# Branch B's head norms: the sum of squares by one product with a tile of ones, power and factor over 256 columns

## The reference, cut to what matters

```python
o_b = hgrn2_chunkwise(qb, 1.0 - f, vb, jnp.log(f)).astype(x.dtype)
o_b = rms_norm(o_b, hgrn_out_norm_g)          # over the 128 channels of each head
y_b = o_b.reshape(B, T, BRANCH_WIDTH) * jax.nn.silu(z_b)

def rms_norm(x, gain):
    xf = x.astype(jnp.float32)
    y = xf * lax.rsqrt(jnp.mean(xf * xf, axis=-1, keepdims=True) + EPS)
    return (y * gain.astype(jnp.float32)).astype(x.dtype)
```

## Time and profile before

| what | value |
|---|---|
| median of 3 runs | 1909.64 us (1907.76 to 1910.26) |
| profiled execution | 1908.92 us, span 1907.6 us |
| granted PE clock, mean | 0.998 of full |
| PE busy | 1890.0 us, 99% of the span |
| PE weight loads busy | 1857.5 us, 97% |
| DVE busy | 1174.7 us, 62% |
| ACT busy | 880.1 us, 46% |
| POOL busy | 323.6 us, 17% |
| PE on the chain that ended last | 92% |

### The profile page before, as it was taken

How to read it: one execution, slowest core, us unless ns; L and a number is a source line. 1 busy time by engine, 2 the same in 40 slices (tenths; PEclk the granted TensorE clock), 3 DMA queues, 4 the chain that set the end, 5 groups by cost and what they waited for, 6 DMA issues and landing times.

```text
span 1907.6 us, 37116 instructions
## 1 busy us (share of the span) xinstructions
PE 1890.0 (99%) x15758; PEld 1857.5 (97%) x15758; DVE 1174.7 (62%) x1709; ACT 880.1 (46%) x1265; POOL 323.6 (17%) x317
## 2 busy tenths in 40 slices
PE   9999999999999999999999999999999999999999
PEld 8999999999999999999999999999999999999987
DVE  7765665656554556755654766676467776655744
ACT  6544454544444444544454543446443333444543
POOL 3220110202110003400221243040011132110300
PEclk9999999999999999999999999999999999999999
DMA  7566555566666666666565565563564444666664
GB/s 262 165 211 182 158 154 165 167 188 191 197 191 195 198 190 188 194 204 193 196 232 195 177 217 168 149 178 119 156 187 140 138 141 142 183 199 195 193 232 154
DMA packets 180752, 347.31 MB, mean 182 GB/s; under 512 B 11742, under 2 KB 24410, under 8 KB 180058
## 3 DMA queue, kind: packets, MB, share of 16 engines
q1 hardware_dynamic: 178938, 340.67, 58.8%
q10 hardware_dynamic: 1648, 4.26, 0.6%
HBM read 334.89 MB, written 6.29 MB: 179 GB/s over the span
## 4 chain that ended last, share of the span: by engine, by line
PE 92%; DVE 3%; SPq 1%; issue 1%; DMA 1%; ACT 1%; POOL 1%; POOLq 0%; ACTq 0%; DVEq 0%
PE bank L1326 91%; DVE w_lo L1973 1%; SPq L1300 1%; DMA scratch<-arena 1%; DMA w_raw<-in_w_in 1%; ACT w_hi L1665 1%; DVE hb L2215 0%; SPq L1259 0%; POOL stats L2533 0%; DVE arena L2079 0%; DVE scratch L2079 0%; ACT L1733 0%; POOL scratch L2583 0%; PE bank L1547 0%; ACT ob L1825 0%
## 5 line engine op out<-in xcount | busy, mean ns | idle before, releaser
L1973 DVE TENSOR_TENSOR w_lo<-w_raw,w_hi 128x1024 fp32r<-128x1024 f32 (+2 forms) x644 | 792.8, 1235 | 460.5 <-ACT w_hi L1665 458.6
L1665 ACT ACTIVATE w_hi<-w_raw 128x1024 fp32r<-128x1024 f32 (+2 forms) x644 | 662.8, 1032 | 854.5 <-PE bank L1326 839.7
L1326 PE MATMUL bank<-hb,w_hi 128*128 128x256 f32 x5284 | 954.5, 278 | 1.7 <-DVE hb L1997 1.6
L1326 PEld LDWEIGHTS bank<-hb,w_hi 128*128 128x128 f32 x5284 | 813.8, 188 | 3.7 <-DVE w_lo L1973 2.2
L1326 PE MATMUL bank<-ob,w_hi 128*128 128x256 f32 (+1 forms) x4060 | 767.7, 283 | 5.0 <-DVE ob L2269 1.7
L1326 PE MATMUL bank<-hb,w_lo 128*128 128x256 f32 x2448 | 677.5, 277 | 0.0
L1326 PEld LDWEIGHTS bank<-ob,w_hi 128*128 128x128 f32 x4060 | 633.2, 188 | 9.1 <-DVE w_lo L1973 2.3
L1326 PE MATMUL bank<-ob,w_lo 128*128 128x256 f32 (+1 forms) x2224 | 621.6, 279 | 0.0
L1326 PEld LDWEIGHTS bank<-hb,w_lo 128*128 128x128 f32 x2448 | 460.9, 188 | 0.0
L1326 PEld LDWEIGHTS bank<-ob,w_lo 128*128 128x128 f32 x2224 | 418.4, 188 | 0.0
L1326 PE MATMUL bank<-w_hi,ob 128*128 128x512 f32 (+1 forms) x384 | 104.4, 359 | 1.0 <-DVE arena L2079 1.0
(11 more groups left out here) (241 smaller groups left out, 1019.6 us busy)
## 6 DMA issues: line engine op xcount, KB each, us to landing
w_raw<-in_w_in SPq DMA_DIRECT2D x436, 512.0 KB, 3.8
w_raw<-in_w_out SPq DMA_DIRECT2D x64, 512.0 KB, 4.2
w_raw<-in_w_o_conv SPq DMA_DIRECT2D x32, 512.0 KB, 4.0
w_raw<-in_w_o_mla SPq DMA_DIRECT2D x32, 512.0 KB, 4.0
w_raw<-in_w_branch SPq DMA_DIRECT2D x32, 512.0 KB, 4.4
w_raw<-in_w_kv_b SPq DMA_DIRECT2D x16, 512.0 KB, 4.6
w_raw<-in_w_q_b SPq DMA_DIRECT2D x16, 384.0 KB, 3.5
arena<-x_kept SPq DMA_DIRECT2D x2, 2048.0 KB, 9.0
```

Of the source, the lines that this page charges most:

```text
L1326: return nc.tensor.matmul(dst, lhsT, rhs, start=start, stop=stop, skip_group_check=True)
L1665: act(dst, src, ACT.Copy).then_inc(S_("w_hi"), 1)
L1973: tt(low, src, high.bitcast(F32), ALU.subtract).then_inc(S_("w_lo"), 1)
```

## The change

The sums are now made by one product: the stationary operand is a 128x128 tile of ones, the moving operand the 256 squares. Each partition of the bank then holds the sums of all 256 tokens. DVE writes mean plus EPS over the squares in the `head_factor` buffer, 128x256; POOL raises all 128x256 numbers to the power -0.5 in place; at the next pump DVE multiplies the head's output by gain and factor, read from the buffer. The second PE step (`row_spread`) and the `stats` buffer are gone, and one side bank is taken for a head where there were two. The number of pumps of the job stays.

```diff
     def out_norm(h, o):
         hd = heads.take()
         s = add("o_sq", h, marks="head_sq", head=hd, o=o)
         yield
-        b, r = yield from row_factor("on", [s["head_sq"]], head=hd)
-        s = add("o_norm", h, marks="o_norm", bank=b, row=r)
-        b.ends(s["o_norm"])
+        b = side.take()
+        s = add("o_sum", h, marks="on_sum on_mean on_pow", bank=b, head=hd, sq=s["head_sq"])
+        b.ends(s["on_mean"])
+        yield
+        s = add("o_norm", h, marks="o_norm", head=hd, power=s["on_pow"])
         hd.ends(s["o_norm"])
# tensor engine
+    def o_sum(s):
+        pe.wait_ge(*s.of["bank"].after)
+        pe.wait_ge(*s.of["sq"])
+        mm(m.side[s.of["bank"].slot][:, 0:S], ones, m.heads[s.of["head"].slot][:, 0:S]).then_inc(S_("on_sum"), 1)
# vector engine
+    def o_sum(s):
+        ve.wait_ge(*s["on_sum"])
+        ts(m.heads[s.of["head"].slot][:, 0:S], m.side[s.of["bank"].slot][:, 0:S], 1.0 / P, EPS,
+           ALU.mult, ALU.add).then_inc(S_("on_mean"), 1)
     def o_norm(s):
         h, = s.args
-        ve.wait_ge(*s.of["row"])
-        stt(m.QB[:, h, :], m.QB[:, h, :], m.col("on"), m.side[s.of["bank"].slot][:, 0:S], ALU.mult, ALU.mult).then_inc(S_("o_norm"), 1)
+        ve.wait_ge(*s.of["power"])
+        stt(m.QB[:, h, :], m.QB[:, h, :], m.col("on"), m.heads[s.of["head"].slot][:, 0:S], ALU.mult, ALU.mult).then_inc(S_("o_norm"), 1)
# general engine
+    def o_sum(s):
+        f = m.heads[s.of["head"].slot][:, 0:S]
+        po.wait_ge(*s["on_mean"])
+        tt(f, f, m.c("neg_half").to_broadcast([P, S]), ALU.pow).then_inc(S_("on_pow"), 1)
```

More of the change, by code:

```diff
@@ L1640, in tensor_engine @@
                 cols=cols, angle=angle, meta_turn=meta_turn, rope_key=rope_key, scores1=scores1, turn1=turn1, mix1=mix1,
-                ki_turn=ki_turn, qa_sum=qa_sum, tok_turn=tok_turn, index=index, scores2=scores2, turn2=turn2,
+                ki_turn=ki_turn, qa_sum=qa_sum, o_sum=o_sum, tok_turn=tok_turn, index=index, scores2=scores2, turn2=turn2,
                 mix2=mix2, rec_diag=rec_diag, rec_level=rec_level, rec_turn=rec_turn, rec_state=rec_state,
@@ L2495, in vector_engine @@
                 rec_diag=rec_diag, rec_scale=rec_scale, rec_level=rec_level, rec_decay=rec_decay, rec_state=rec_state,
-                o_norm=o_norm, out2=out2)
+                o_sum=o_sum, o_norm=o_norm, out2=out2)
     for s in plan.steps:
@@ L2623, in rec_scale @@
         tt(left(m.kL), left(m.kK), left(m.Rb), ALU.mult).then_inc(S_("rec_left"), 1)
-    does = dict(clear_meta=clear_meta, constants=constants, x_tile=x_tile, latent=latent, out1=out1, row_sum=row_sum, qa_sum=qa_sum, rope=rope,
+    does = dict(clear_meta=clear_meta, constants=constants, x_tile=x_tile, latent=latent, out1=out1, row_sum=row_sum, qa_sum=qa_sum, o_sum=o_sum, rope=rope,
                 rr=rr, bgate=bgate, zconv=zconv, z_gate=z_gate, merge=merge, x1_square=x1_square,
```

## The result

The changed kernel took 2223.72 us, median of 4 runs (2222.55 to 2224.43), the kernel before beside it 1909.33 us. The ratio is 1.1647, 95% interval 1.1627 to 1.1667: 314 us slower. The prediction said 2217 us (2130 to 2253). The profiled execution has a span of 2222.0 us.

The account below looks back on a forecast made before the run. PE's own work was taken to bound the kernel (busy 99%). 1908.9 us + 288.8 for stops behind POOL's powers - 3.6 saved on PE + 23.2 for the clock = 2217.3, said as 2217 us, range 2130 to 2253.

Parts of the forecast that it names:

- PE's saving: On PE, two narrow products replaced by one of 256 columns: 0.45 us a head, 3.6 us for 8 heads (2.8 to 4.0).
- The power's price: On POOL, the line from one to three columns extended to 256: 39.7 us for each power.
- the upper level of 0.9 us: On POOL, a second duration level of powers and products, 0.9 us higher; as a bound, 40.6 us for a power.
- The covers: Time from a power's start until its delay stops PE, less the steps between: 28.8 us off eight powers' 317.6.
- What PE waits for: Eight PE waits of 30 to 39 us: first three pairs ended by POOL `left`, last by DVE `w_lo` or a read-out.
- The clock: PE at 1.2 GHz after each of eight stops: 2.9 us each, 23.2 us in all (0 to 30).
- The sum: Whole kernel: 1908.9 + 288.8 - 3.6 + 23.2 = 2217.3 us, 16% slower.
- The bend of the line: Rival: POOL's powers are cheaper by the column over many columns; 2060 us at half the slope; chance 0.14.
- the price of a product: Rival: POOL's power costs like a product, 0.73 to some 3 us, PE never stops, 1905.3 us; chance 0.06 with another rival.
- full exposure: Rival: stops cost more than the power less its cover; with no cover at all 2253 us; chance 0.05.
- The threshold of the third: Powers on POOL under about 3.3 us, the shortest distance (4.2 - 0.85), would never stop PE.
- The 1.6 us: First pair's second head: DVE's backlog after the first stop makes the cover of 5.0 us 1.6 us shorter.

Follow-up runs that it names:

- version with full clock: Changed kernel plus 74 to 101 unread 256-column products on PE per head, so PE rests under 1 us in each stop by plan; 2219.55 us.
- version with the power alone: Kernel before plus an unused 128x256 power on POOL behind each of its eight 128x2 powers; 2189.47 us, ratio 1.1468.
- root version: Changed kernel with the power off POOL: ACT takes the square root, DVE the reciprocal; three runs, ratios 0.9997, 0.9988, 0.9985.
- the extra products: Changed kernel plus 74 unread 256-column products of constants on PE after each head's gain step; 2221.69 us.
- ln and exp: Changed kernel with the power moved from POOL to ACT as exp(-0.5 ln x), two instructions over 128x256; 1907.53 us, ratio 0.9991.

## Why the prediction was right, and where its terms were off

It named the cause, the price within 5%, the eight stops and what ends them, and the total within 7 us of 314. Two of its terms were wrong by 16 us each, in opposite directions, so the total is closer than the working deserves: that part is luck.

- **PE's saving, 3.6 us.** With the power's length taken away 2.6 us are left by the medians, 0.6 to 3.8 by the interval. 3.6 is inside, at the upper end.
- **The power's price, 39.7 us each.** Right in kind, 5% short: the mean is 41.7, eight of them 333.7 us and not 317.6. Two things are in it: 0.159 us a column where the first three sizes gave 0.1535, which is 1.4 us, and the upper level of 0.9 us in most heads, which I had kept as a bound. The Trainium skill (GPSIMD Engine Reference, section Elementwise — side-by-side cycle accounting) gives 2.6 cycles for each element of a two-input operation. That fits the product's row and not the power's 0.159 us a column, which are, as an estimate at that page's 1.2 GHz clock, 190 cycles.
- **The covers, 28.8 us in all.** In the version with full clock each power moves the next one by X less its cover, and against the pairs' first powers in the kernel before (1466.38, 1511.87, 1558.46 and 1604.51 us) the pairs' covers, PE's saving in them, are 7.1, 7.4, 4.3 and 7.9 us, 26.6 together. Predicted were 7.2, 7.2, 6.1 and 8.3 with the saving of 3.6 beside them, 32.4. So they were read 5.8 us too long, 2.7 of it in the third pair. Within a pair the split was off as well: in the first pair 3.1 and 4.0 us, where 4.5 and 2.7 were predicted beside the saving of 0.9, so that the pair's 7.1 comes nearer than its two parts.
- **What PE waits for.** Six stops by `left`, then one by `w_lo` and one by a read-out: as forecast, place by place, and all but the last (40.2) within the forecast 30 to 39 us. The version with the power alone shows that POOL's queue does the first six.
- **The clock, 23.2 us.** Wrong in size: 7.2 us by the spans, 4 by the medians, with the spread named above. The step that failed is the multiplication by eight. The low clock came after every stop, 0.50 to 0.75 in the windows behind them, and PE's busy time did grow by 19 us, but after the first stop of each pair PE's time is not what the next power waits for: DVE's row of steps is 5.45 us at either clock. Slow instructions there only shorten the next rest.
- **The sum.** 16.1 us more for the powers, 5.8 us less cover, 16.0 us less for the clock: 2217.3 + 5.9 = 2223.2 us, where 2223.3 were measured. This closes by construction and proves nothing: the covers are what is left of the span with full clock, and the clock's term is the rest to the changed kernel's span. How the two share 34 us hangs on one execution, the faster of the two with full clock.
- **The rivals.** The bend of the line, the price of a product, and full exposure are all excluded by runs. The threshold of the third was set too high: 3.3 us, from the third pair's first head, where a power of 3.08 us did not stop PE. It is about 2.6 us and lies at the second heads, where a power of 2.89 us stopped PE for 0.6 us. The 1.6 us by which the prediction shortened a second head's cover, and only after a stop, are there without one: 3.4 us in place of 5.0.
- **Left open:** why the root version keeps about half of PE's saving. Its waits of PE are no longer than before (1.7 us at most behind the kernel's first 20 us), and the intervals are as wide as the question.

## What to carry to other kernels

Price an operation on each engine by its own rows and by its size: two columns of a power here cost as much as 256 of a product, and three small sizes gave the large one within 5%. On an engine that runs in order, ask what stands behind the long instruction and not who needs its result. When a sum has a term for every stop, check for each stop that the engine slowed down is the one that sets the time until the next event.

## What was not expected of the hardware

- POOL's power is a straight line from 3 columns to 256: 0.85 us for 3 columns, 2.89 for 16, 20.72 for 128, 41.12 for 256.
- After rests of 3.8 to 6.3 us behind the extra products, some 32 us of dense work, the clock was at 1.2 GHz when PE went on or 0.3 us later; with rests of 2.2 us and less in the second version it stayed at 2.4 GHz.
- DVE's reciprocal over 128x256 took 1.75 us, four times the 0.42 us of a multiply and add of the same size.
- ACT has 10 table loads of 1.28 us in the kernel before, 18 with the root and 30 with ln and exp: 4 and 16 of the new ones stand at the new functions, 4 at others that had to be loaded again. None of it showed in the time.
